# All rows of x loaded and turned at the start, and the head norms' reciprocals taken by way of DRAM

## The reference, cut to what matters

```python
mod = jax.nn.silu(c) @ w_ada[l] + b_ada[l]
shift1, scale1, gate1, shift2, scale2, gate2 = jnp.split(mod, 6, axis=-1)
h = rms_norm(x, norm1_g[l]) * (1.0 + scale1[:, None, :]) + shift1[:, None, :]
z = h @ w_in[l]
```

```python
d_out = (rms_norm(d_out, subln_g[l]) * (1.0 - lambda_init)).reshape(b, s, DIFF_HEADS * DIFF_V_DIM)
mix = jnp.concatenate([mla_out, d_out], axis=-1) @ w_out[l]
x = x + gate1[:, None, :] * mix
h2 = rms_norm(x, norm2_g[l]) * (1.0 + scale2[:, None, :]) + shift2[:, None, :]
```

## Time and profile before

| | |
|---|---|
| median of 3 runs | 2505.71 us (2505.2 to 2509.43) |
| profiled execution | 2508.09 us, span of the trace 2506.4 us |
| PE busy | 2315.1 us, 92% |
| DVE busy | 1826.0 us, 73% |
| ACT busy | 1279.8 us, 51% |
| mean granted TensorE clock | 0.963 |
| first block, start to the last latent product | 0 to 92.7 us |
| output block | 655 to 803 us |

### The profile page before, as it was taken

How to read it: one execution, slowest core, us unless ns; L and a number is a source line. 1 busy time by engine, 2 the same in 40 slices (tenths; PEclk the granted TensorE clock), 3 DMA queues, 4 the chain that set the end, 5 groups by cost and what they waited for, 6 DMA issues and landing times. The chain is left out here.

```text
span 2506.4 us, 31726 instructions
## 1 busy us (share of the span) xinstructions
PE 2315.1 (92%) x10602; PEld 1865.9 (74%) x10602; DVE 1826.0 (73%) x2210; ACT 1279.8 (51%) x1723; POOL 523.9 (21%) x482
## 2 busy tenths in 40 slices
PE   6989997988887699999999689999999999999997
PEld 5767765777665588888888568887877888887886
DVE  6588885666676799999999775454357666664988
ACT  4366664566522588888888551111653333333444
POOL 1662000885010111111110200000024233223000
PEclk8999997999898799999999799999999999999999
DMA  7352121339365899999999844333323223237442
GB/s 255 90 159 55 44 91 44 96 109 328 120 207 183 312 412 411 412 411 412 412 412 411 348 157 138 121 113 132 96 68 92 75 78 98 75 126 258 154 143 110
DMA packets 238062, 486.64 MB, mean 194 GB/s; under 512 B 21635, under 2 KB 127568, under 8 KB 237202
## 3 DMA queue, kind: packets, MB, share of 16 engines
q1 hardware_dynamic: 204194, 365.71, 40.7%
q0 software_dynamic: 27440, 98.62, 11.7%
q10 hardware_dynamic: 6336, 21.11, 2.1%
HBM read 403.30 MB, written 76.56 MB: 191 GB/s over the span
## 5 line engine op out<-in xcount | busy, mean ns | idle before, releaser
L2490 ACT ACTIVATE e_w<-e_raw 128x1024 fp32r<-128x1024 f32 x384 | 406.7, 1062 | 121.0 <-PE e_pgu L113 59.0
L2426 DVE TENSOR_TENSOR e_w<-e_raw,e_w 128x1024 fp32r<-128x1024 f32 x384 | 450.9, 1222 | 16.5 <-ACT e_w L2490 10.4
L113 PE MATMUL e_pgu<-e_w,e_xt 128*128 128x512 f32 x1536 | 360.7, 395 | 4.2 <-DVE e_xt L2434 4.2
L113 PEld LDWEIGHTS e_pgu<-e_w,e_xt 128*128 128x128 f32 x1536 | 288.2, 189 | 64.2 <-DVE e_xt L2434 2.8
L113 PE MATMUL s_ps<-h,s_w 128*128 128x512 f32 x1152 | 266.8, 392 | 3.8 <-DVE h L2866 3.8
L113 PEld LDWEIGHTS s_ps<-h,s_w 128*128 128x128 f32 x1152 | 215.7, 188 | 50.2 <-DVE h L2866 5.1
L113 PE MATMUL w_ps<-w_out,w_ring 128*128 128x512 f32 x1056 | 244.1, 390 | 2.2 <-DVE w_ring L3658 2.2
L113 PEld LDWEIGHTS w_ps<-w_out,w_ring 128*128 128x128 f32 x1056 | 198.2, 188 | 45.0 <-DVE w_out L3665 3.0
L113 PE MATMUL w_ps<-w_out 128*128 128x512 f32 x924 | 211.7, 392 | 2.7 <-DVE w_out L3852 2.6
L113 PEld LDWEIGHTS w_ps<-w_out 128*128 128x128 f32 x924 | 174.5, 189 | 39.8 <-DVE w_out L3850 3.0
L113 PE MATMUL w_ps<-y,w_ring 128*128 128x512 f32 x816 | 196.0, 398 | 4.3 <-ACT w_h L3424 3.0
(11 more groups left out here) (481 smaller groups left out, 4078.3 us busy)
## 6 DMA issues: line engine op xcount, KB each, us to landing
e_raw<-in_w_expert_gate_dram SPq DMA_DIRECT2D x128, 512.0 KB, 12.5
e_raw<-in_w_expert_up_dram SPq DMA_DIRECT2D x128, 512.0 KB, 11.9
e_raw<-in_w_expert_down_dram SPq DMA_DIRECT2D x128, 512.0 KB, 12.3
w_raw<-in_ffn_w_gate_up_dram SPq DMA_DIRECT2D x48, 512.0 KB, 6.1
y_rows<-am_zrow SPq DMA_DIRECT2D x4, 4352.0 KB, 33.5
y_rows<-e_yo ACTq DMA_DIRECT2D x32, 512.0 KB, 6.7
section_rows<-in_ada_w_dram POOLq DMA_DIRECT2D x32, 512.0 KB, 3.9
raw_rows<-in_w_ada_dram POOLq DMA_DIRECT2D x24, 512.0 KB, 3.9
```

Source lines behind the costliest of these rows:

```text
L113: o = pe.matmul(out, stat[i], mov[j], start=start and n == 0, stop=stop and n == 2)
L2426: dve.tensor_tensor(w[1][:, slot % CUT], raw[:, slot], w[0][:, slot % CUT].bitcast(F32), ALU.subtract).then_inc(low, 1)
L2490: act.activation(w[0][:, slot % CUT], raw[:, slot], ACT.Copy).then_inc(high, 1)
```

## The change

In the first block all eight blocks of x are loaded before the sections. ACT takes squares and root of one block, DVE the reciprocal (now 128x1), and ACT multiplies the rows by it in place (`scale_x`) before PE turns them. So `rbc`, the four-wide diagonal and `spread_roots` go, DVE's multiplication becomes one with two scalars (`modulate`), and all eight copies out of PSUM are DVE's; ACT made six of them. `latents` starts when all eight blocks are turned and the first columns are there, and takes both halves of the tokens of one k together.

```diff
-        ORDER = [(k, hf) for hf in range(2) for k in range(HK)] + [(k, 2) for k in range(HK, KD)]
+        ORDER = [(0, 0), (0, 1)] + [(k, 2) for k in range(1, KD)]
...
-                for n in range(4):
+                for n in range(NT):
                     sp.dma_start(x_rows[:, n, :], x_v[n]).then_inc(x_in[n], 16)
-                for t in range(KD):
+                for t in range(4):
...
                 load_lat_w(0)
-                for n in range(4, NT):
-                    sp.dma_start(x_rows[:, n, :], x_v[n]).then_inc(x_in[n], 16)
-                for t in range(4):
+                for t in range(4, KD):
+                    load_section(0, t)
+                for t in range(KD):
                     load_section(1, t)
                 load_lat_w(1)
-                for t in range(4, KD):
-                    load_section(1, t)
                 sp.dma_start(g.cs[:], a["const_rope"].rearrange("s p t -> p s t")).then_inc(cs_in, 16)
-                sp.wait_ge(spread, NT)
+                sp.wait_ge(unit_done, NT)
...
                 def turn_x(n):
-                    pe.wait_ge(x_in[n], 16)
-                    if n >= 4:
-                        pe.wait_ge(x_copied, n)
-                    elif n >= 2:
+                    pe.wait_ge(unit_done, n + 1)
+                    if n >= 2:
                         pe.wait_ge(x_copied, n - 1)
                     for k in range(KD):
-                        o = pe.transpose(x_turn_at(n)[:, k // HK, k % HK * P:(k % HK + 1) * P], x_rows[:, n, k * P:(k + 1) * P], g.ident[:])
+                        o = pe.transpose(ps[:, n % 2, k * P:(k + 1) * P], x_rows[:, n, k * P:(k + 1) * P], g.ident[:])
...
                 def latents():
 
-                    pe.wait_ge(rb_copied, 1)
-                    pe.wait_ge(vec_ready, 1)
-                    pe.wait_ge(x_copied, 4)
-                    for k in range(HK):
+                    pe.wait_ge(mod_ready, 1)
+                    for k in range(HK - 1):
                         pe.wait_ge(lw_low, k + 1)
-                        pe.wait_ge(h_low, ORDER.index((k, 0)) + 1)
-                        for c in range(4):
-                            latent(k, c, 0)
-                        turn_x(4 + k)
-                    spread_roots(1)
-                    pe.wait_ge(x_copied, NT)
-                    pe.wait_ge(rb_copied, 2)
-                    for c in (1, 2, 3):
-                        for k in range(HK):
-                            pe.wait_ge(h_low, ORDER.index((k, 1)) + 1)
-                            latent(k, c, 1)
+                        for hf in range(2):
+                            pe.wait_ge(h_low, ORDER.index((k, 2 if k else hf)) + 1)
+                            for c in range(hf, 4):
+                                latent(k, c, hf)
+                    pe.wait_ge(lw_low, HK)
+                    pe.wait_ge(h_low, ORDER.index((HK - 1, 2)) + 1)
+                    for c in (2, 3):
+                        for hf in range(2):
+                            latent(HK - 1, c, hf)
                     section(1)
+                    latent(HK - 1, 0, 0)
+                    for hf in range(2):
+                        latent(HK - 1, 1, hf)
```

ACT's and DVE's functions in the first block:

```diff
+                def square_root(n):
+                    act.wait_ge(sq, n + 1)
+                    act.activation(root[:, n:n + 1], ssx[:, n:n + 1], ACT.Sqrt, bias=g.eps[:], scale=1.0 / D).then_inc(rt, 1)
+
+                def scale_x(n):
+                    act.wait_ge(inv, n + 1)
+                    act.activation(x_rows[:, n, :], x_rows[:, n, :], ACT.Copy, scale=rstd[:, n:n + 1]).then_inc(unit_done, 1)
...
-                    act.activation(h_t[0][:, k, part], full[:, k, part], ACT.Identity, bias=g.mod[:, 0, k:k + 1]).then_inc(h_high, 1)
+                    act.activation(h_t[0][:, k, part], full[:, k, part], ACT.Copy).then_inc(h_high, 1)
...
                 square(0)
-                for n in range(3):
-                    square(n + 1)
-                    copy_x(n)
-                square_roots(0)
-                copy_x(3)
-                copy_roots(0)
+                square_root(0)
+                for n in range(NT):
+                    if n < NT - 1:
+                        square(n + 1)
+                        square_root(n + 1)
+                    scale_x(n)
...
+                def inverse(n):
+                    dve.wait_ge(rt, n + 1)
+                    dve.reciprocal(rstd[:, n:n + 1], root[:, n:n + 1]).then_inc(inv, 1)
...
-                    dve.scalar_tensor_tensor(out=full[:, k, spans[hf]], in0=full[:, k, spans[hf]], scalar=g.a_col[:, k:k + 1], in1=rbc[:, spans[hf]],
-                                             op0=ALU.mult, op1=ALU.mult).then_inc(affine, 1)
+                def modulate(j):
+                    k, part = ORDER[j][0], spans[ORDER[j][1]]
+                    dve.tensor_scalar(full[:, k, part], full[:, k, part], g.a_col[:, k:k + 1], g.mod[:, 0, k:k + 1], ALU.mult, ALU.add).then_inc(affine, 1)
 
                 def h_rest(j):
                     k, part = ORDER[j][0], spans[ORDER[j][1]]
                     dve.wait_ge(h_high, j + 1)
-                    dve.scalar_tensor_tensor(out=h_t[1][:, k, part], in0=full[:, k, part], scalar=g.mod[:, 0, k:k + 1], in1=h_t[0][:, k, part].bitcast(F32),
-                                             op0=ALU.add, op1=ALU.subtract).then_inc(h_low, 1)
+                    dve.tensor_tensor(h_t[1][:, k, part], full[:, k, part], h_t[0][:, k, part].bitcast(F32), ALU.subtract).then_inc(h_low, 1)
```

```diff
+        hcol = sb("hcol", [P, HEADS, NT])
+        pick = sb("pick", [P, 2, 2])
...
+                for p in range(2):
+                    two = slice(2 * p, 2 * p + 2)
+                    pool.wait_ge(rooted, p + 1)
+                    pool.dma_start(g.head_root_dram[two], acc[0:2, p, :]).then_inc(root_out, 16)
+                    pool.wait_ge(root_out, 16 * (p + 1))
+                    pool.dma_start(hcol[:, two, :], by_column(g.head_root_dram[two])).then_inc(col_in, 16)
+                    pool.wait_ge(inv, p + 2)
+                    pool.dma_start(by_column(g.head_inv_dram[two]), hcol[:, two, :]).then_inc(inv_out, 16)
+                    pool.wait_ge(inv_out, 16 * (p + 1))
+                    for j in range(2):
+                        if p:
+                            pool.wait_ge(done, j + 1)
+                        pool.dma_start(root[:, j, :], g.head_inv_dram[2 * p + j].partition_broadcast(P)).then_inc(inv_row[j], 16)
...
-                    if h:
-                        pe.wait_ge(rooted, h)
+                    if h == 0:
+                        pe.wait_ge(inv, 1)
+                    elif h == 2:
+                        pe.wait_ge(rooted, 1)
                     for cols in halves:
-                        o = pe.matmul(spot[:, cols], g.ones[:], sq[:, h % 2, cols], start=True, stop=True)
+                        o = pe.matmul(spot[0:2, cols], pick[:, h % 2, :], sq[:, h % 2, cols], start=(h % 2 == 0), stop=(h % 2 == 1))
...
                 head_squares(0)
+                head_squares(1)
                 for k in range(KD):
                     pe.wait_ge(w_low, k + 1)
                     if k >= HEADS:
                         pe.wait_ge(b_low, k - HEADS + 1)
                     for n in range(3):
                         product(n, k)
-                    if k < HEADS - 1:
-                        head_squares(k + 1)
-                    elif HEADS <= k < KD - 1:
+                        if k == 0 and n == 1:
+                            head_squares(2)
+                            head_squares(3)
+                    if HEADS <= k < KD - 1:
                         row(k - HEADS)
...
-                def square_root(h):
-                    act.wait_ge(ssq, h + 1)
-                    if h >= 2:
-                        act.wait_ge(done, h - 1)
-                    act.activation(root[:, h % 2, :], spot, ACT.Sqrt, bias=g.eps[:], scale=1.0 / P).then_inc(rooted, 1)
+                def square_roots(p):
+                    act.wait_ge(ssq, 2 * p + 2)
+                    act.activation(acc[0:2, p, :], spot[0:2, :], ACT.Sqrt, bias=g.eps[0:2, :], scale=1.0 / P).then_inc(rooted, 1)
...
+                for i in range(3):
+                    row(i)
...
+                def inverses(p):
+                    dve.wait_ge(col_in, 16 * (p + 1))
+                    dve.reciprocal(hcol[:, 2 * p:2 * p + 2, :], hcol[:, 2 * p:2 * p + 2, :]).then_inc(inv, 1)
...
-                    dve.wait_ge(inv, h + 2)
+                    if h == 0:
+                        dve.wait_ge(inv, 1)
+                    dve.wait_ge(inv_row[h % 2], 16 * (h // 2 + 1))
...
+                for h in range(2):
+                    dve.memset(pick[:, h, h:h + 1], 1.0)
+                    dve.memset(pick[:, h, 1 - h:2 - h], 0.0)
...
-                modulate(0)
+                for n in range(6):
+                    modulate(n)
                 take(0)
```

(42 more changed lines are left out.)

193 lines of the change are left out of this document (47 added, 146 removed).

## The result

The changed kernel takes 2527.74 us (median of 4 runs, 2524.97 to 2530.67) beside 2507.57 of before: ratio 1.0085, interval 1.0071 to 1.0099, 20 to 21 us slower. The forecast was 2514 and the range ended at 2521; the sign was right, the size and the range were not.

A forecast was written before the change was run, and what follows sets the result against it. PE, busy nine tenths of the span, was taken as the bound, with loading up to 32 us. First block +4.6 and output block +4.0 gave +8.6 us on the median 2505.71, so 2514, range 2506 to 2521.

The forecast's parts named there:

- 14.4 us later at the first product: First block: scaling, turning and copying all eight blocks moves the first latent product from 32.18 to 46.6.
- 10.4 given back: First block: turns 3.4, spreading of roots 1.16, waits 4.3 and slow restart 1.5 leave PE's path, 10.4 us.
- a new wait of 0.6: First block: PE waits 0.6 us, between 0 and 3, at the second columns while DVE adds eight sections.
- Again 2.7 + 4.9: Output block, second pair's trip: 2.7 us out to DRAM and 4.9 into all partitions, in at 692.9.
- rival three: Second trip meets SP's router loads and DVE starves PE at the second columns: +8 and +7, 2521; chance 0.12.
- one rest of `w_out` later: Output block: two normalisations, two rests and this rest, 6.2 us, put DVE's second reciprocal at 685.3.
- ACT's copy at gate row 1: Output block: PE waits for ACT's copy of row 0, standing 7 us; +1.3 us at the end of k = 7.
- the 6.9 us that the block could win: Output block: PE's waits before k = 6 and k = 7 and slow products, 1.2 + 4.1 + 1.6.
- DVE's order: Output block: pieces ahead of the takes delay the second logits from 760.66 to 764.6, +3.9 us.
- Output block +4.0: Whole output block 4.0 us slower, with bounds of -2.5 and +8.
- The upper bound of +8: Output block: worst case, with trips of 3.5 + 6 us.
- Rival one: Output block: short trips of 1.5 + 3.8 a pair, row's copy done before PE asks; +2.1, 2507.8; chance 0.22.

The follow-up runs named there:

- e9: New first block alone, old output block, with POOL's first two subtractions moved behind the sections, against the kernel before: ratio 1.0021.
- e6: e5 with the gain row and router loads held back until the second pair's rows landed, against the kernel before: ratio 0.9996.
- e7: Kernel before with only heads 2 and 3 going through DRAM, gain row and router loads held back, against the kernel before: 2501.16 us, ratio 0.9980.
- e3: e2 with SP's gain row and router loads held back until the second pair's rows landed, against the kernel before: ratio 1.0063.
- e5: e4 with ACT's copies of the gate rows put ahead of the leading parts again, against the kernel before: ratio 1.0023.
- e4: e2 with DVE's modulation pieces and takes in the order of the kernel before, against the kernel before: ratio 1.0049.
- e2: The output block's edit alone, first block as before, against the kernel before: ratio 1.0071.

## Why the prediction was wrong

**First block: the sum right by luck.** Forecast: 14.4 us later at the first product (46.6), 10.4 given back, a new wait of 0.6, so +4.6 and the next stage at 96 to 98. Measured: 16.7 later (48.85), 12.5 given back with the new wait of 0.68 taken off, so +4.2 and 96.88. The start came 2.2 later than forecast: POOL's collision with the sections (2.0 us, e9) was counted for the later subtractions and left out for the first two. The give-back, 9.8 with the wait taken off, was larger by 2.7. Of these 1.7 stand in a row that the forecast did not count, the 12 products behind the second columns before:

```profile
66.47 4.61 PE L113 MATMUL ad_po<-h,m_lat_w 128*128 128x512 f32 x12 [0.26 <-DVE mod L1043]
```

They took 4.61 us at a granted clock of 0.63 (66.4 to 71.0), partly at the lower level; the changed kernel's 12 at 72.38 took 2.89, and its clock was 1.00 from 70.2 to 75.1. The edit does not decide this: e6 and e7, with the first block of before, took 3.02, and e9, with a new one, had 0.72. So two errors of over 2 us, one of them a matter of the execution, cancelled.

**The failed step: the trip's price.** "Again 2.7 + 4.9" put 7.6 us on each pair. With the gain row and the router's loads held back it is 8.4 to 8.6 until the rows are in use (second trips of e6 and e3, still beside the eighth load of `w_out`), and the first pair's first normalisation began after 9.1. The second trip was taken at the same 7.6 and took 13.5 and 16.0 for its two rows. The collision stood in rival three only, with a chance of 0.12, and yet it is built in: SP's gain row and router loads wait for the sixth rest of `w_out`, and DVE's second reciprocal stands directly behind that rest in the new order. The forecast's sum followed that very rest ("one rest of `w_out` later") without adding what else it releases. e6 prices it at 6.2 us.

**What followed was right, and longer.** PE does wait for ACT's copy at gate row 1, 12.3 us instead of 7, and the 6.9 us that the block could win are used up; with the place of ACT's copies given back, 4.5 us go (e5). Head 0's rest was late as well, 2.31 us before k = 4, where the forecast had PE arrive without a wait.

**DVE's order: mechanism right, somewhat small.** Behind the end of k = 7 the forecast had 2.7 us more (4.0 less 1.3); measured are 4.9 (14.7 less 9.8, the delay of k = 7's end) in the changed kernel and 3.8 by e4.

**The sum.** Output block +4.0 forecast, +14.7 measured; of the 10.7 between them 8.5 stand at the end of k = 7 (9.8 against 1.3) and 2.2 behind it. The upper bound of +8 took 3.5 + 6 for a trip. Rival one needed trips under about 4.2 us a pair. The Trainium skill's fit for POOL's transfers (DMA: Bandwidth & Descriptors, Anatomy of one DMA) gave an estimate of 5.2 for the two steps; the traces have 8.4 to 8.6 where only the eighth load of `w_out` runs beside them (e6, e3), and the measurement decides. The range was too narrow because rival three was priced as a mishap, while in all four kernels with this order and without SP's wait (the changed one, e2, e4, e5) the second trip took 12.6 to 13.6 us to its first row in use.

## What to carry to other kernels

Before pricing a trip through memory, look at which instruction releases it and what else that instruction releases: here the trip and SP's loads, let go by one instruction of DVE, met in all four kernels. A long latency costs nothing only where the work behind it has slack: here two trips for the four heads win nothing even at their best (e6: a stretch of 146.2 against 146.7), and one for the two heads whose products come last wins 6.6 (e7: 140.1). A copy that frees a PSUM tile for PE should not stand behind work that waits for memory.

## What the runs showed of the hardware

POOL's 128x512 subtractions beside DVE's fused multiply-add on 128x512 stretched it from 0.68 us an instruction (2.73 for four) to 1.19 (4.76 for four). The Trainium skill (SBUF — State Buffer, SBUF: two separate sides) has the two engines exclude each other for a whole instruction, where DVE reads two inputs from SBUF and POOL reads there too; the trace comes close: POOL's two alone take 2.49 (e9, below), all six one after another would take 5.22, and they took 4.81 (32.45 to 37.26).

```profile
41.47 2.49 POOL L286 TENSOR_TENSOR m_lat_w<-m_lat_raw_w,m_lat_w 128x512 fp32r<-128x512 f32 x2 [40.92 <-ACT m_lat_w L712]
```

After the store of 128x16 values POOL's next issue waited 1.50 us in e7, 2.99 in e3 beside the eighth load of `w_out`, and 4.84 in the changed kernel beside SP's ten loads. A row store issued on POOL's queue right behind two 512 KB row loads (681.05) released POOL only 4.27 us later, where the first one, alone, took 1.50:

```profile
667.53 0.54 POOL L1660 DMA_DIRECT2D head_roots<-po_macc  x1 [59.49 <-ACT po_macc L1809]
669.57 0.76 POOL L1662 DMA_DIRECT2D po_hcol<-head_roots  x1 [1.50 <-DMA head_roots<-po_macc]
...
681.05 0.52 POOL L1660 DMA_DIRECT2D head_roots<-po_macc  x1
685.84 0.75 POOL L1662 DMA_DIRECT2D po_hcol<-head_roots  x1 [4.27 <-DMA head_roots<-po_macc]
690.64 0.73 POOL L1664 DMA_DIRECT2D head_inverses<-po_hcol  x1 [4.06 <-DVE po_hcol L1891]
696.21 1.08 POOL L1669 DMA_DIRECT2D po_root<-head_inverses  x2 [4.84 <-DMA head_inverses<-po_hcol]
```
